# Lower weight parts of the second MLP product: negated ScalarE copies and accumulating transfers in place of GpSimd subtractions

## The reference, cut to what matters

```python
h = rmsnorm(x, norm1_g) * (1 + sc1) + sh1
x = x + g1 * mixer(h)                    # w_in, pooling, short conv, conformer, w_out
h = rmsnorm(x, norm2_g) * (1 + sc2) + sh2
x = x + g2 * (square(relu(h @ w_ff1)) @ w_ff2)
y = rmsnorm(x, final_g)
```

## Time and profile before

| | us |
|---|---|
| median of three runs | 1076.5 |
| profiled execution, its own time | 1077.4 |
| its span from first to last instruction | 1075.6 |
| PE busy in the span | 1038.0 (97%) |
| DVE busy | 873.0 (81%) |
| ACT busy | 407.0 (38%) |
| POOL busy | 273.0 (25%) |

### The profile page before, as it was taken

One profiled execution on the slowest core, in us unless ns is written; L12 is line 12 of the kernel. 1 busy time (PEld: TensorE's weight loads), 2 busy tenths in 40 slices (PEclk: granted clock), 3 DMA queues, 4 the chain that ended last, 5 costly groups with the idle time before them and its releaser, 6 DMA issues.

```text
span 1075.6 us, 19292 instructions
## 1 busy us (share of the span) xinstructions
PE 1038.0 (97%) x7843; PEld 1007.3 (94%) x7843; DVE 873.0 (81%) x1235; ACT 407.0 (38%) x584; POOL 273.0 (25%) x236
## 2 busy tenths in 40 slices
PE   6899999999999799999999999999999999999996
PEld 5688899999999698999999999999999999999996
DVE  5899899998466986967767767779988988988866
ACT  6321111111232464655555555473333333333221
POOL 3742122222212500000000000044545545545500
PEclk8899999999989988999999999999999999999999
DMA  9967411211114121653453453487655445425312
GB/s 282 344 233 294 167 45 32 59 33 37 37 43 131 79 93 45 186 173 115 148 174 113 150 158 131 150 258 229 191 140 149 151 140 148 131 81 189 107 51 108
DMA packets 112769, 148.62 MB, mean 138 GB/s; under 512 B 6465, under 2 KB 78088, under 8 KB 110617
## 3 DMA queue, kind: packets, MB, share of 16 engines
q1 hardware_dynamic: 111928, 146.15, 42.7%
q0 software_dynamic: 336, 0.58, 0.2%
q10 hardware_dynamic: 417, 0.65, 0.2%
HBM read 110.40 MB, written 37.44 MB: 137 GB/s over the span
## 4 chain that ended last, share of the span: by engine, by line
PE 79%; DVE 15%; issue 3%; DMA 1%; ACT 1%; SPq 1%; DVEq 0%; ACTq 0%
PE banks L2334 29%; PE banks L2448 24%; PE banks L2106 18%; DVE plain L1431 4%; PE banks L2488 3%; DVE split L1645 1%; DMA plain<-in_w_ada 1%; PE banks L2137 1%; DVE split L1900 1%; PE banks L2201 1%; PE banks L2223 1%; DVE plain L1450 1%; PE banks L2520 1%; PE banks L2126 1%; DVE xT L1944 0%
## 5 line engine op out<-in xcount | busy, mean ns | idle before, releaser
L2334 PE MATMUL banks<-split 128*128 128x262 f32 x2688 | 336.2, 288 | 2.3 <-DVE gate_s L1491 1.2
L2334 PEld LDWEIGHTS banks<-split 128*128 128x128 f32 x2688 | 333.8, 192 | 4.6 <-DVE gate_s L1491 1.7
L2448 PE MATMUL banks<-split 128*128 128x258 f32 x2352 | 283.3, 283 | 3.4 <-DVE xT L1944 1.6
L2448 PEld LDWEIGHTS banks<-split 128*128 128x128 f32 x2352 | 282.5, 189 | 4.0 <-issue 2.1
L836 POOL TENSOR_TENSOR split<-plain,split 128x512 fp32r<-128x512 f32 x103 | 156.5, 1543 | 478.6 <-ACT split L1056 478.6
L2106 PEld LDWEIGHTS banks<-split 128*128 128x128 f32 x1656 | 264.6, 191 | 12.5 <-issue 7.1
L2106 PE MATMUL banks<-split 128*128 128x344 f32 x1656 | 268.8, 324 | 6.7 <-DVE gate_s L1491 6.1
L1056 ACT ACTIVATE split<-plain 128x1024 fp32r<-128x1024 f32 (+1 forms) x120 | 112.5, 948 | 174.1 <-PE banks L2448 138.2
L1947 DVE TENSOR_TENSOR xT<-xT,banks 128x516 f32<-128x516 f32 x180 | 123.1, 686 | 28.4 <-PE banks L2448 23.4
L1431 DVE SCALAR_TENSOR_TENSOR plain<-plain 128x1023 f32<-128x1023 f32 (+14 forms) x90 | 136.3, 1514 | 2.9
L777 POOL TENSOR_TENSOR split<-plain,split 128x1024 fp32r<-128x1024 f32 (+2 forms) x29 | 65.7, 2266 | 247.0 <-ACT split L889 247.0
(11 more groups left out here) (236 smaller groups left out, 811.2 us busy)
## 6 DMA issues: line engine op xcount, KB each, us to landing
plain<-hid_home SPq DMA_DIRECT2D x106, 262.0 KB, 3.4
hid_home<-xT SPq DMA_DIRECT2D x102, 262.0 KB, 3.5
plain<-in_w_ff SPq DMA_DIRECT2D x18, 1024.0 KB, 6.5
plain<-in_w_ada SPq DMA_DIRECT2D x16, 1024.0 KB, 7.4
plain<-in_w_ff SPq DMA_DIRECT2D x56, 256.0 KB, 3.9
plain<-in_w_in SPq DMA_DIRECT2D x17, 512.0 KB, 6.2
plain<-in_w_ada SPq DMA_DIRECT2D x16, 512.0 KB, 6.8
plain<-in_x_prompt SPq DMA_DIRECT2D x8, 512.0 KB, 8.2
```

Source lines behind the costliest of these rows:

```text
L2334: last = nc.tensor.matmul(banks[:, bank + t, 0:width], weight(p, w, i), operand(p, x, pieces[n], t, width), start=(p in FIRST_OF_CHAIN and ...
L2448: last = nc.tensor.matmul(banks[:, bank + t, 0:QT], weight(p, h, 2 * kb + jj), halves(queue_piece(e, x))[:, t, 0:QT], start=(p in FIRST_OF ...
```

## The change

In the second product ACT writes, right behind each upper part, the same source a second time into the tile of the lower part, scaled by -1 and so rounded as the upper part is. POOL no longer subtracts. It waits for that copy and issues a transfer which adds the source onto the tile, so that the tile ends as source minus upper part. The four lower parts of a unit now have one semaphore each (`down_lo[g]`, 16 for each transfer), and every wait on `split_lo` behind unit UP is rewritten: PE's four, SP's before a raw buffer is loaded again, DVE's before the mixed blocks are overwritten, ACT's before the last late split. The first product and the late part keep their subtractions.

```diff
+        down_neg = sem("down_neg")
+        down_lo = [sem(f"down_lo{g}") for g in range(4)]
...
                 elif unit == 1:
                     sp.wait_ge(oper_lo, len(LO_ORDER))
+                elif unit < UP + 2:
+                    sp.wait_ge(split_lo, split_at(unit - 2, 2))
                 else:
-                    sp.wait_ge(split_lo, split_at(unit - 2, 2))
+                    sp.wait_ge(down_lo[0], 16 * (unit - UP - 1))
+                    sp.wait_ge(down_lo[2], 16 * (unit - UP - 1))
...
             def load_late(unit):
                 h = unit - UP - 2 * GROUPS
-                sp.wait_ge(split_lo, 4 * unit - 5)
+                sp.wait_ge(down_lo[0], 16 * (unit - UP - 1))
+                sp.wait_ge(down_lo[2], 16 * (unit - UP - 1))
...
-            sp.wait_ge(split_lo, 4 * (UP + 2 * GROUPS) + 2)
+            sp.wait_ge(split_lo, 4 * UP + 2)
...
             for unit in range(UP, UP + 2 * GROUPS):
                 for g in range(4):
-                    low_split(unit, g)
+                    pool.wait_ge(down_neg, 4 * (unit - UP) + g + 1)
+                    pool.dma_start(split_of(g, 1), split_source(unit, g), accum_op=ALU.add).then_inc(down_lo[g], 16)
...
                 nc.scalar.activation(split_of(g, 0), src, ACT.Copy).then_inc(split_hi, 1)
+                if unit >= UP:
+                    nc.scalar.activation(split_of(g, 1), src, ACT.Copy, scale=-1.0).then_inc(down_neg, 1)
...
                 if j == 3:
-                    act.wait_ge(split_lo, 4 * unit)
+                    act.wait_ge(down_lo[1], 16 * (unit - UP))
+                    act.wait_ge(down_lo[3], 16 * (unit - UP))
...
                     dve.wait_ge(raw_loaded[unit % 2], raw_at(unit))
-                    dve.wait_ge(split_lo, 4 * unit)
+                    dve.wait_ge(split_lo, 4 * min(unit, UP))
+                    if unit > UP:
+                        dve.wait_ge(down_lo[1], 16 * (unit - UP))
+                        dve.wait_ge(down_lo[3], 16 * (unit - UP))
...
-                        dve.wait_ge(split_lo, 4 * (UP + 2 * GROUPS) + 4)
+                        dve.wait_ge(split_lo, 4 * UP + 4)
...
                 if jj == 0 and p in (0, 3, 5, 6):
-                    pe.wait_ge(split_lo, split_at(unit, (0, 3, 5, 6).index(p)))
+                    pe.wait_ge(down_lo[(0, 3, 5, 6).index(p)], 16 * (unit - UP + 1))
...
                 if q == 0:
-                    pe.wait_ge(split_lo, 4 * (UP + 2 * GROUPS) + j + 1)
+                    pe.wait_ge(split_lo, 4 * UP + j + 1)
```

## The result

The change makes the kernel slower: 1110.35 us (median of 4 runs, 1103.71 to 1117.81) against 1076.86 us of the kernel before (4 runs, 1073.62 to 1079.33), a ratio of 1.0309 with a 95% interval of 1.0236 to 1.0381. The forecast was 1103 us, in a range from 1073 to 1150. The profiled execution took 1115.04 us, its span 1113.2 us.

A forecast was written before the change was run, and what follows sets the result against it. PE was taken to bound the kernel, saturated for most of the second product. Median 1076.5 us plus 29.9 us of waits for transfers minus 3.3 us gained at the start gave 1103.1 us, range 1073 to 1150.

The forecast's parts named there:

- 29.9 us of waits for transfers: Second product: PE waits 2.3 us a unit for late lower parts, over 13 units, the first unit excepted.
- POOL's subtractions were hidden: Second product: 98 POOL instructions, 148.9 us, off PE's path in the steady state; removing them by itself gives nothing.
- The gain of 3.3 us at the start: All of PE's waits in the second product, nearly all near its start, would go; bounds 0 and 4.4 us.
- the conflict: Start of second product: DVE slows beside POOL; four `queue_low` take 4.74 us, against 2.54 with POOL mostly idle.
- ACT's 48 us are covered: Second product: ACT's added copies over 14 units fit its free time, as it is busy 7.5 us of 20.
- this as a rival: ACT's copies make ACT late, so queue entries come late; no chance of its own, as 9 us of 20 are free.
- Two passes, 8.8 us to landing: Each 512 KB addition reads source and destination through the same engines: 0.5 + 1.3 + 7.0 us; chance 0.42.
- the two ends, one and two passes: Landing of an addition: 5.3 us if it costs no more than a copy, 8.8 us if the destination is read too.
- Group 1 is the tight one, 2.3 us in each unit: Group 1's lower part has 6.5 us from issue to PE's read, the shortest gap; landing at 8.8 is 2.3 late.
- Issue or movement growing with the pieces: POOL's issue grows to 4.6 us for 1024 pieces of 512 bytes, costing 64 us; within the slow-queue rival, chance 0.25.
- The hidden loads behind SP's wait are met by the ring, save near the end: SP's hidden loads, some 6 us later behind its wait for group 2, still arrive in time, except near the end.

The follow-up runs named there:

- the run with plain copies: The changed kernel with POOL's 56 transfers as plain copies, the addition left out: 1084.07 us, 1.0056 to the kernel before.
- the run with the copies alone: The kernel before with ACT's 56 negated copies added, each ahead of POOL's subtraction, which is kept and waits for it: 1083.1 us, ratio 1.0056.
- the whole pieces: The changed kernel with transfers of groups 0 and 2 reading another same-size tile, so all pieces are 4 or 2 KB: 1091.4 us, 1.0140 to the kernel before.

## Why the prediction was right, and where it was off

The direction and the mechanism held: additions beside the other traffic, landing too late for single-buffered tiles with short gaps. That the total came so near is in part luck. The forecast had 29.9 us of waits for transfers, at steps 0 and 3 of thirteen units; PE's waits for them were 19.2 us, 4.6 of them in the first unit, for which it had none. The rest is waits for gathers (11 us, 6 of them near the end, where hidden loads came late) and slower matmuls (12.6 us), neither of them in the sum. By its steps:

- *POOL's subtractions were hidden, so removing them gives nothing on PE's path.* Right. Their end gave DVE its time back (one `queue_low` 698 ns in the mean, 925 before), and PE did not gain from it.
- *The gain of 3.3 us at the start.* Wrong. In the run with plain copies, where the conflict is gone, PE still waits 2.7 us on DVE's gathers at the start (and 8.3 us in the whole stage), and holding POOL back mostly moved the waits. So the conflict alone does not make them; that the order of DVE's list at that place does was not tested.
- *ACT's 48 us are covered.* Wrong, by up to 6 us as the run with the copies alone has it. I compared busy time with free time over a unit; what counted, as the waits have it, was which instruction stands behind the copy in ACT's list. The forecast had named this as a rival and given it no chance.
- *Two passes, 8.8 us to landing.* The size was too high in the median: 7.3 us, with landings up to 15.0. Of the two ends, one and two passes, the traces lie between: an addition's packets take 1.39 times as long as a copy's at 512 bytes, 1.75 times at 4 KB. That a second read of the destination is the reason is not shown.
- *Group 1 is the tight one, 2.3 us in each unit.* This step failed. I gave all four groups the same time per byte and the same traffic beside them, and so looked at the shortest gap. Of the 19.2 us PE waits 17.1 at step 0 for group 0, 1.5 at step 7 for group 2 and 0.6 at step 3 for group 1. Group 1 landed in its 6.5 us in the median (6.4); group 0, in pieces of 512 bytes and beside the loads that SP issues in front of it, took 8.6 and up to 14.8 us where the forecast left it 8.0. The stalls are a few long ones, where the raw load and eight hidden loads meet group 0, with small ones between.
- *Issue or movement growing with the pieces* stood among the rivals with 64 us, as an issue of 4.6 us. The issue did grow, to 1.57 us against 0.88 for the whole pieces, not to 4.6, and with it the time of the packets (eight of 512 bytes 536 ns, one of 4 KB 332).
- *The hidden loads behind SP's wait are met by the ring, save near the end.* Right in both halves: near the end SP waits for group 2 at the late raw load until 1005.48 us, the last four hidden loads go out at 1008.11, ACT waits 9.4 us for the first, and DVE's gather ends PE's wait of 6.1 us. It was named and not priced.
- *Clock.* Not in the sum: after each long wait PE works for some us at half the clock (0.50 granted), which costs about 2 us for a wait of 5 and some 7 us in all, as estimated above.

The Trainium skill's page "Collectives: The Full Stack" (The bandwidth ceiling) gives a reducing transfer, with its two source reads, about half the rate of a copy. These traces agree that an addition costs the engines more than a copy, though 1.39 to 1.75 times as much and not twice. By the Trainium skill's page "DMA: Bandwidth & Descriptors" (Anatomy of one DMA) 512 KB would land in an estimated 3.2 us; plain copies took 4.6 and additions 7.3 us here, beside other traffic.

Of the 33.5 us lost, by the ratios and in this order of taking away: the small pieces 18, the additions in whole pieces 9, the transfers as such nothing that can be told, the copies 6. In another order the shares would differ, since cutting the hidden loads gives back 21 us with the small pieces still there. These are differences of runs on several chips, each with some 3 to 8 us of uncertainty. With the hidden loads cut an addition in small pieces still takes 6.0 us to land, which is early enough for nearly every read; what the traffic adds to that, from about 1 us in the median to 9, was not followed packet by packet.

## What to carry to other kernels

An engine that is hidden is worth nothing to the time, and work taken from it has to go somewhere with a shorter deadline in hand: compare the deadline of each tile with the landing of the new transfer at the load of that stage, with its pieces as well as its bytes, and beside what the other queue sends at that moment. A free share of an in-order engine says little; look at what stands behind the added instruction and who waits for it. And where a transfer's landing also starts the next loads, a late landing can move these loads into the way of the next transfer.

## What the runs showed of the hardware that was not expected

- An accumulating transfer of 512 KB in pieces of 512 bytes took 1.57 us to issue and landed after 7.5 us in the median beside all the other traffic, after 6.0 us with the hidden loads cut; in pieces of 4 KB it took 0.86 to 0.89 us and landed after 5.7 to 6.4. A plain copy from the same queue: 0.89 us to issue in pieces of 512 bytes, 0.54 in pieces of 4 KB, and 4.5 to 4.7 to land.
- Packets of GpSimd's queue between two tiles on the chip, mean in the second product: 512 bytes 67 ns as an addition and 48 as a copy, 2 KB 184 and 130, 4 KB 332 and 189. SyncE's loads of weights from HBM took 28 ns for 512 bytes and 56 for 1 KB.
- An addition of GpSimd's queue, issued 3 us behind a load of 1 MB on the hardware queue and beside 2 MB more of it, landed after 13.5 us.
- After 4.9 us without a matmul the granted clock stood at 0.50 for the next 3.9 us, and at 0.97 in the 5 us after these.
